# Two fused transformer blocks in one kernel: new SBUF offsets for the activation tiles

## The reference

```python
# block 1
hn = rmsnorm(x, norm_mix_g); proj = hn @ w_in            # 1024 x 3592
fox = decayed causal attention(8 heads of 64); rec = hgrn2 recurrence(4 heads of 128)
h = x + concat(fox, rec) @ w_out
h = h + cross_attention(rmsnorm(h), rmsnorm(mem)) @ w_xo  # w_xq, w_xkv
h = h + square(relu(rmsnorm(h) @ w1)) @ w2                # 4096 wide
x2 = rmsnorm(h, final_norm_g)
# block 2
proj = rmsnorm(x2) @ w_in_2                               # q, k, v, pool, memory q, 3 gates
mix = g0 * (diff_attention @ w_a) + g1 * (pool @ w_p) + g2 * (memory attention @ w_m)
x = x2 + rmsnorm(mix @ w_out_2)
up = causal_conv3(rmsnorm(x) @ w_up_2)                    # 2 x 2816 wide
out = x + rmsnorm((gelu(up_g) * up_v) @ w_down_2)
```

## Time and profile before

| | us |
|---|---|
| median of 3 executions | 934.35 |
| the three | 939.44, 934.35, 934.3 |
| the profiled execution | 939.44 |
| its span, first to last instruction | 937.7 |

### The profile page before, as it was taken

The page is one execution under the profiler, slowest core; times in us unless marked ns, Lnnn a source line. Parts: engine busy times, 40 slices in busy tenths (PEclk is TensorE's granted clock), DMA queues, the critical chain, the costliest instruction groups (busy, mean ns, idle before and its releaser), DMA issues.

```text
span 937.7 us, 16025 instructions
## 1 busy us (share of the span) xinstructions
PE 913.3 (97%) x6412; PEld 842.6 (90%) x6412; DVE 580.0 (62%) x762; ACT 496.5 (53%) x725; POOL 98.8 (11%) x148
## 2 busy tenths in 40 slices
PE   6999999999999999999989999999999999999997
PEld 6998998887987999988879988999999899999885
DVE  4674576654644766644365348868587588887643
ACT  5774645544654654533364446765543666666531
POOL 7202122200001000000040006001000200000000
PEclk9999999999999999999999999999999999999999
DMA  7865523225433665565527554444555476665641
GB/s 244 273 228 187 180 92 133 92 94 175 161 110 106 194 205 191 182 214 187 185 96 226 186 175 134 156 159 157 179 181 181 113 206 190 186 179 181 216 141 45
DMA packets 134803, 157.52 MB, mean 168 GB/s; under 512 B 3752, under 2 KB 113566, under 8 KB 134750
## 3 DMA queue, kind: packets, MB, share of 16 engines
q1 hardware_dynamic: 133085, 151.78, 50.7%
q0 software_dynamic: 1056, 3.93, 1.1%
q10 hardware_dynamic: 608, 1.06, 0.3%
HBM read 155.71 MB, written 1.05 MB: 167 GB/s over the span
## 4 chain that ended last, share of the span: by engine, by line
PE 89%; DVE 4%; ACT 3%; issue 1%; POOL 1%; DMA 1%; SPq 0%; DVEq 0%; POOLq 0%; ACTq 0%
PE tb L567 17%; PE tb L569 16%; PE tb L568 16%; PE acc L567 10%; PE acc L568 10%; PE acc L569 10%; PE tb L645 1%; DMA raw<-in_w_in 1%; PE acc L750 1%; ACT junk L1089 1%; DVE wlo L1485 1%; ACT whi L1062 1%; DVE xlo L1498 0%; PE tb L842 0%; PE acc L973 0%
## 5 line engine op out<-in xcount | busy, mean ns | idle before, releaser
L1485 DVE TENSOR_TENSOR wlo<-raw,whi 128x2048 fp32r<-128x2048 f32 (+1 forms) x143 | 326.8, 2289 | 239.6 <-ACT whi L1062 239.5
L567 PE MATMUL tb<-xhi,whi 128*128 128x256 f32 x1256 | 352.6, 281 | 0.6 <-DVE xlo L1498 0.3
L568 PE MATMUL tb<-xlo,whi 128*128 128x256 f32 x1256 | 350.1, 279 | 0.0
L569 PE MATMUL tb<-xhi,wlo 128*128 128x256 f32 x1256 | 350.0, 279 | 0.0
L1062 ACT ACTIVATE whi<-raw 128x2048 fp32r<-128x2048 f32 (+1 forms) x143 | 272.4, 1910 | 134.5 <-PE acc L569 112.0
L567 PEld LDWEIGHTS tb<-xhi,whi 128*128 128x128 f32 x1256 | 236.4, 188 | 1.9 <-issue 1.3
L569 PEld LDWEIGHTS tb<-xhi,wlo 128*128 128x128 f32 x1256 | 237.8, 189 | 0.0
L568 PEld LDWEIGHTS tb<-xlo,whi 128*128 128x128 f32 x1256 | 236.1, 188 | 0.1
L465 POOL TENSOR_SCALAR rs<-ss 128x1 f32<-128x1 f32 x16 | 7.6, 478 | 412.0 <-ACT junk L1089 411.7
L569 PE MATMUL acc<-whi,hid_lo 128*128 128x512 f32 x128 | 49.8, 389 | 0.0
L568 PE MATMUL acc<-wlo,hid_hi 128*128 128x512 f32 x128 | 49.8, 389 | 0.0
(11 more groups left out here) (330 smaller groups left out, 1404.7 us busy)
## 6 DMA issues: line engine op xcount, KB each, us to landing
raw<-in_w_in SPq DMA_DIRECT2D x42, 1024.0 KB, 5.1
raw<-in_w SPq DMA_DIRECT2D x32, 1024.0 KB, 5.2
raw<-in_w_up SPq DMA_DIRECT2D x44, 512.0 KB, 5.0
raw<-in_w_down SPq DMA_DIRECT2D x22, 512.0 KB, 4.0
raw<-in_w_xkv SPq DMA_DIRECT2D x8, 1024.0 KB, 5.3
raw<-in_w_out SPq DMA_DIRECT2D x8, 1024.0 KB, 5.0
raw<-in_w_mem_kv SPq DMA_DIRECT2D x4, 1024.0 KB, 5.1
raw<-in_w_xq SPq DMA_DIRECT2D x4, 1024.0 KB, 5.1
```

The lines of the kernel that those rows point to most:

```text
L567: pe.matmul(o, a_hi, b_hi, start=start, stop=False)
L568: pe.matmul(o, a_hi, b_lo, start=False, stop=False)
L569: return pe.matmul(o, a_lo, b_hi, start=False, stop=stop)
L1485: dve.tensor_tensor(wlo[:, n % RING, :m], raw[:, n % RING, :m], whi[:, n % RING, :m].bitcast(F32), ALU.subtract).then_inc(lo_ready, 1)
```

## The change

Five sizes and six start offsets change: both rooms are 128 B shorter, the homes in them other than rec's start at 12 elements (48 B) instead of 48 (192 B), `gap` is 32 B instead of 160, `gap_m` 64 B instead of 192, and a new `gap_l` of 64 B stands ahead of `lvl`. No instruction is added, removed or moved.

```diff
-        xhi_room = sb("xhi", [P, KT * T + 64], F32R)
-        xlo_room = sb("xlo", [P, KT * T + 64], F32R)
+        xhi_room = sb("xhi", [P, KT * T + 32], F32R)
+        xlo_room = sb("xlo", [P, KT * T + 32], F32R)
...
-        sb("gap", [P, 40])
+        sb("gap", [P, 8])
...
-                sb("gap_m", [P, 48], at=r1)
+                sb("gap_m", [P, 16], at=r1)
                 mhi = sb("mhi", [P, KT, T], F32R, at=r1)
                 mlo = sb("mlo", [P, KT, T], F32R, at=r1)
+                sb("gap_l", [P, 16], at=r1)
                 lvl = sb("lvl", [P, 7, P], at=r1)
...
-        START = {"x": 48, "rec": 0, "h1": 48, "h2": 48, "x2": 48, "a": 48, "h4": 48}
+        START = {"x": 12, "rec": 0, "h1": 12, "h2": 12, "x2": 12, "a": 12, "h4": 12}
```

## The result

| | before | changed | ratio (95% interval) |
|---|---|---|---|
| median, us | 936.57 (4 executions) | 950.28 (4) | 1.0144 (1.0102 to 1.0186) |
| lowest to highest | 934.3 to 939.44 | 948.41 to 951.83 | |
| span of the profiled execution | 937.7 | 948.0 | |

The forecast was 929.7 us with a range of 921 to 948. The measured time lies above the range. Over all 32 executions of the kernel before, those beside the experiments included, the median is 938.15 us; against that the change is 1.3% slower.

What follows compares the result with a forecast made beforehand. TensorE was taken to bound the kernel: number of matmuls times the distance between starts. From the profiled 939.44 us, 9.2 (x streams) and 0.5 (x as stationary) came off, the other terms 0, giving 929.7 us, range 921 to 948.

Steps and rivals of the forecast that it cites:

- Term 1: The 3768 256-column matmuls that stream xhi/xlo: slow stretches turn quick, 9.2 us off.
- Term 3: w2, w3, xo and w_down, 840 matmuls now 128 B off modulo 256: loss between 0 and 5.0 us, taken as 0.
- Term 2: x as stationary tile, in fv to gg and vd: 0.5 us off.
- term 4: ScalarE and VectorE writing xhi and xlo at the new alignment: at most 1.0 us, taken as 0.
- the slower one: Every 256-column stage on xhi disturbed at 48 B, 4.6 ns each: 947.6 us; chance 0.25.
- The redraw rival: Offset does nothing, paces drawn again at each restart: 934.3 us, some runs at 939.4; chance 0.27.
- The signs: A third matmul duration anywhere would show the mechanism wrong; w1, quick before, at 281 ns the sign wrong.

Runs made afterwards that it cites:

- e4: Kernel before with only START changed, a different offset for each use of the x rooms (0 to 160 B); one execution, 952.27 us.
- e3: Kernel before with START 12 alone, rooms as before, xhi and xlo both at 48 B; 950.65 us, ratio 1.0113.
- e7: Kernel before with START 28 (112 B) for all names but rec, nothing else; 932.48 us against 937.79, ratio 0.9948.
- e2: Kernel before with the change's shorter rooms and START alone, gap tiles as before; 947.05 us, ratio 1.0086.
- e1: Kernel before with the change's gap tiles alone, rooms and START as before; 944.76 us against 939.53, ratio 1.0061.
- e6: Kernel before with an unused 128 B tile ahead of all others, every address moved, no distance; one execution, 938.91 us beside 938.03.

## Why the prediction was wrong

**What bounds: right.** The distance between starts accounts for about 8.9 of the 10.3 us between the two spans, and a short stretch of lower clock in the changed one for the rest. The two paces at one address, and their size (4.6 ns), were read rightly; the spread of the kernel before, 933.5 to 944 us over 32 executions, lies within the 17 us that such draws can make of 3768 matmuls by 4.6 ns. What decides a draw stays open.

**Term 1 failed by its sign.** It was put at 9.2 us less, and the x streams came out at about 3.2 us more (3.4 + 0.4 + 0.3 - 0.8 - 2.4 + 1.4 + 0.9). The step was: "48 lies on the side of the quick rows". It joined two things that the rows didn't join. The quick rows at 0 B were matmuls with x-like tiles as the stationary side and 512 columns; with x streaming, 0 B is at 119.9 ns (e4), among the slowest. And 192 B isn't an edge with quick ground beside it: 176 and 208 B are both slow. At 48 B there is no quick pace (e3). The term also counted modulo 128 B, where `xhi` and `xlo` move alike; modulo 256 B they part, to 48 and 176 B, and the third pace comes with that. The sum for all quick, 929.7, was sound as arithmetic: the layout in which every x stream is quick (e7) has 932.5. Of the 2.8 us missing about 1.2 is x as stationary, of whose excess I had taken half off and which in e7 pays in full, 240 matmuls by 7 ns; some 0.7 is the 768 matmuls from up to ga at about 1 ns over the quick pace. The rest wasn't split further.

**Term 3 was mis-sized.** I bounded it by 0 and 5.0 us and took 0, guessing a pattern that repeats by 128 B. For w2, 256 B make no difference (e2) and 128 B do (e1), and the 840 matmuls cost 4.8 us, nearly the upper bound. In the same sentence of the layout stood `phi` and `ohi`, which also moved modulo 256 B, and I gave them no price: 0.8 us. `wo` had none either: with the shorter room its `xlo` lies 128 B past a multiple, 0.4 us.

**Term 2 and term 4** were small: vd fell by 0.3 us and fv to gg grew by 0.15, and the waits for the fills stayed as they were. That the clock has no part was right of the kernel before; in the profiled execution of the changed one it cost 1.5 us.

**The rival that came true** was the slower one: every x stage disturbed, 947.6 us, with term 3 on top 953. Measured were 950.28, between the two, since qd and kd, cv and six slabs from up to ga ran at a third pace that I had put in no case (115.5). It had a chance of 0.25, and the range ended at 948 because term 3's bound was not carried into the upper end of the rival that it could join. The redraw rival, that the offset does nothing, is refuted: w2 had one pace in all layouts with a distance of 0 and another at 128 B.

**The signs** that the prediction named for being wrong both came: third durations (395 ns in w2; 277, 278 and 280 in cv), and w1, quick before, at 281.

**The two independent read ports** of the Trainium skill ("TensorE: Matmul & The Clock Gate", step by step), by which loading weights costs the running matmul nothing, don't account for these runs, and the measurement decides: the rule leaves no room for the distance, but moving only one of the two tiles by 128 B took w2 from 226.7 to 233.0 ns (e1), moving both left it at 226.4 (e6). That it is the weight load that the stream meets, and not the drain or something in the array, is my reading; no run separated these.

## What to carry to other kernels

When a kernel is bound by a dense stream of matmuls, put the starts of one stage beside those of another with the same shapes: two paces at one clock are a sign that the placement of the two operands in SBUF matters, here worth 113.3 to 121.9 ns a matmul, over 7%. Don't reason about such offsets; measure them, with one kernel that gives each stage another offset, and write down what the layout must keep: here the distances modulo 256 B, which shorter padding tiles changed for stages that the edit didn't name. A kernel whose repeated executions spread widely may be drawing between paces, and a distance at which no draw is seen can lower the spread as well as the median, as 112 B did here. And before a difference between two profiled executions is put down to the change, look through windows for short stretches of a lower clock: the page's tenths hid one of 3.6 us.

## What was not expected of the hardware

- The distance between the moving and the stationary tile modulo 256 B changes the spacing of fp32r matmuls: 226.7 ns at 0 B and 232.4 at 128 B for 512 columns; 113.3 to 121.9 for 256. Moving all tiles by 128 B together changed no pace (e6).
- At 192 B one and the same stage runs at 113.3 or at 117.8 ns and keeps it through up to 1056 matmuls; 16, 144 and 208 B have two paces as well. At 112 B only 113.4 to 115.0 ns were seen, at 104 and 120 B 120.0 and 121.9.
- One distance isn't good for every stage: 0 B is the quickest with x stationary (vd 226.5, 512 columns) and among the slowest with x streaming (119.9, 256 columns). Whether the role or the number of columns makes this no run separated.
